# Four token-half seams: the new layer's first weight tile gets its own place and is split ahead of the norm, and the second half's root goes ahead of the second split

## The reference

```python
def rms_norm(x, w=None):
    y = xf * lax.rsqrt(jnp.mean(xf * xf, axis=-1, keepdims=True) + EPS)
def ada_in(x, g, m, s):
    return rms_norm(x, g) * (1 + m[:, 3 * s + 1][:, None, :]) + m[:, 3 * s][:, None, :]
def swiglu(h, w_in, w_out):
    g, u = jnp.split(h @ w_in, 2, axis=-1)
    return (jax.nn.silu(g) * u) @ w_out
...
    for l in range(DEPTH):      # 2; the context stream likewise, with m_ctx
        x = x + 0.5 * ada_gate(m_lat, 0) * swiglu(ada_in(x, norm_w[l, 0], m_lat, 0), ...)
        hl = ada_in(x, norm_w[l, 1], m_lat, 1)
        yc, yl = ab_mixer(...) if l % 2 == 0 else ret_mixer(...)   # DeltaNet || differential attention; retention
        x = x + ada_gate(m_lat, 1) * yl
        x = x + 0.5 * ada_gate(m_lat, 2) * swiglu(ada_in(x, norm_w[l, 2], m_lat, 2), ...)
    return rms_norm(x, final_norm_w)
```

## Time and profile before

| | us |
|---|---|
| median of 3 runs (2037.15 to 2040.97) | 2037.5 |
| the profiled execution: its own time | 2038.63 |
| the profiled execution: span from first to last instruction | 2036.8 |
| PE busy | 1988.5 (98%) |
| DVE busy | 1282.7 (63%) |
| ACT busy | 751.9 (37%) |
| mean granted TensorE clock | 0.989 of full speed |

### The profile page before, as it was taken

One profiled execution on the slowest core, in us unless ns is written; L12 is line 12 of the kernel. 1 busy time (PEld: TensorE's weight loads), 2 busy tenths in 40 slices (PEclk: granted clock), 3 DMA queues, 4 the chain that ended last, 5 costly groups with the idle time before them and its releaser, 6 DMA issues.

```text
span 2036.8 us, 27638 instructions
## 1 busy us (share of the span) xinstructions
PE 1988.5 (98%) x10253; PEld 1687.3 (83%) x10255; DVE 1282.7 (63%) x1840; ACT 751.9 (37%) x990; POOL 109.3 (5%) x165
## 2 busy tenths in 40 slices
PE   9999999999999999999999999999999999989998
PEld 7888888886788888888888888888887888878886
DVE  6877678775648775877677753453346632666666
ACT  5321222345444333332222343212235432746453
POOL 1010011000003200100001000000000000000000
PEclk8999999999999999999999999999999999999999
DMA  8555455521210002555555432352234422044553
GB/s 349 168 198 177 163 202 166 185 96 40 88 68 21 1 22 104 196 186 174 180 193 172 161 123 98 98 176 103 65 101 167 149 98 104 21 165 137 173 187 122
DMA packets 52650, 274.80 MB, mean 135 GB/s; under 512 B 6128, under 2 KB 7472, under 8 KB 34256
## 3 DMA queue, kind: packets, MB, share of 16 engines
q1 hardware_dynamic: 33024, 203.97, 28.8%
q0 software_dynamic: 18960, 68.88, 10.2%
q10 hardware_dynamic: 576, 0.69, 0.1%
HBM read 272.47 MB, written 1.05 MB: 134 GB/s over the span
## 4 chain that ended last, share of the span: by engine, by line
PE 91%; DVE 5%; ACT 3%; issue 1%; DVEq 0%; ACTq 0%
PE ps L1020 15%; PE ps L1022 14%; PE ps L1021 14%; PE ps L1032 8%; PE ps L1250 6%; PE ps L1252 6%; PE ps L1251 6%; PE ps L1033 4%; PE ps L2397 2%; PE ps L2399 2%; PE ps L2398 2%; PE ps L1902 1%; DVE w_lo L682 1%; PE ps L1914 1%; PE ps L2483 1%
## 5 line engine op out<-in xcount | busy, mean ns | idle before, releaser
L682 DVE TENSOR_TENSOR w_lo<-w_raw,w_hi 128x2048 fp32r<-128x2048 f32 (+3 forms) x206 | 420.8, 2043 | 199.9 <-ACT w_hi L461 199.4
L1020 PE MATMUL ps<-h_parts,w_lo 128*128 128x512 f32 (+1 forms) x1424 | 537.1, 377 | 5.4 <-DVE h_parts L841 4.4
L1022 PE MATMUL ps<-h_parts,w_hi 128*128 128x512 f32 (+1 forms) x1424 | 534.3, 375 | 0.0
L1021 PE MATMUL ps<-h_parts,w_hi 128*128 128x512 f32 (+1 forms) x1424 | 534.2, 375 | 0.0
L461 ACT ACTIVATE w_hi<-w_raw 128x2048 fp32r<-128x2048 f32 (+3 forms) x207 | 354.1, 1710 | 451.8 <-PE ps L1252 254.0
L690 DVE SCALAR_TENSOR_TENSOR ada_product<-ada_w,silu_c 128x1024 bf16<-128x1024 f32 x256 | 313.1, 1223 | 20.3 <-DVE ada_product L690 10.5
L1020 PEld LDWEIGHTS ps<-h_parts,w_lo 128*128 128x128 f32 x1424 | 268.4, 188 | 54.8 <-DVE w_lo L682 5.0
L1022 PEld LDWEIGHTS ps<-h_parts,w_hi 128*128 128x128 f32 x1424 | 268.3, 188 | 48.7
L1021 PEld LDWEIGHTS ps<-h_parts,w_hi 128*128 128x128 f32 x1424 | 268.5, 189 | 47.4
L473 ACT ACTIVATE sil<-ps 128x512 f32<-128x512 f32 x66 | 39.5, 598 | 480.5 <-PE ps L1022 480.5
L1250 PE MATMUL ps<-hid_parts,w_lo 128*128 128x512 f32 x468 | 182.1, 389 | 0.0
(11 more groups left out here) (337 smaller groups left out, 2547.7 us busy)
## 6 DMA issues: line engine op xcount, KB each, us to landing
w_raw<-in_w_up SPq DMA_DIRECT2D x88, 1024.0 KB, 4.8
ada_w<-in_ada POOLq DMA_DIRECT2D x128, 512.0 KB, 3.6
w_raw<-in_w_down SPq DMA_DIRECT2D x32, 768.0 KB, 4.2
w_raw<-in_w_down SPq DMA_DIRECT2D x32, 640.0 KB, 3.9
w_raw<-in_w_ret_t SPq DMA_DIRECT2D x16, 1024.0 KB, 4.8
w_raw<-in_w_ab SPq DMA_DIRECT2D x14, 1024.0 KB, 4.8
ada<-in_ada SPq DMA_DIRECT2D x8, 1024.0 KB, 25.4
w_raw<-in_w_ret SPq DMA_DIRECT2D x8, 1024.0 KB, 4.8
```

The lines of the kernel that those rows point to most:

```text
L682: dve.tensor_tensor(w_lo[parts_of(s, slot)][:, 0:elems], w_raw[slot][:, 0:elems], w_hi[parts_of(s, slot)][:, 0:elems].bitcast(F32), ALU.su ...
L1020: pe.matmul(out, lo, rhs_hi(k), start=first and k == 0, stop=False)
L1021: pe.matmul(out, hi, rhs_lo(k), start=False, stop=False)
L1022: mm = pe.matmul(out, hi, rhs_hi(k), start=False, stop=last and k == nk - 1)
```

## The change

The high and low parts of tile s6 + 2 of each seam get the third pair of buffers (`SEAM_FIRST`), so their making no longer waits for PE to leave a slot: `split_hi` waits for `step_done` s − 2 there. That `split_hi` now stands right behind the dummy root that loads ACT's table, ahead of the squares, and that `split_lo` between the second place of half 0 and the reciprocal. In the rest of the seam `low`s and scales alternate from the start. `split_hi` of tile s6 + 3 stands behind the fourth shift instead of the eighth, `split_lo` of it behind the second half's reciprocal instead of ahead of it (at n11 still ahead). On PE the second part of the second half's sum comes one k later.

```diff
+    SEAM_FIRST = tuple(R[name][1] for name in ("diff", "up1a", "up2a", "retg"))
     def parts_of(s, slot):
-        return 2 if isinstance(s, int) and s == 2 else slot
+        return 2 if isinstance(s, int) and s in (2,) + SEAM_FIRST else slot
...
-            act.wait_ge(step_done, s - 1)
+            act.wait_ge(step_done, s - 2 if isinstance(s, int) and s in SEAM_FIRST else s - 1)
...
         act.activation(warm_root[:], vecs[:, 2:3], ACT.Sqrt).then_inc(warmed, 1)
+        split_hi(act, s6 + 2, s6 % 2, ELEMS[s6 + 2])
         for i in range(2):
             act.wait_ge(sq_added, adds_before(norm) + TAIL - 2 + i)
             square(0, i)
         root(0)
-        split_hi(act, s6 + 2, s6 % 2, ELEMS[s6 + 2])
-        for c in range(4):
+        for c in range(3):
             shift(0, c)
         square(1, 0)
+        shift(0, 3)
+        split_hi(act, s6 + 3, (s6 + 1) % 2, ELEMS[s6 + 3])
         shift(0, 4)
-        shift(0, 5)
         square(1, 1)
-        shift(0, 6)
-        shift(0, 7)
-        split_hi(act, s6 + 3, (s6 + 1) % 2, ELEMS[s6 + 3])
+        for c in range(5, KD):
+            shift(0, c)
         root(1)
...
             place(0, i)
+        split_lo(dve, s6 + 2, s6 % 2, ELEMS[s6 + 2])
         dve.wait_ge(mod_ready, k)
         inverse(0)
         scale(0, 0)
         scale(0, 1)
+        low(0, 0)
         dve.wait_ge(step_done, s6 + 1)
         place(1, 0)
         scale(0, 2)
+        low(0, 1)
         scale(0, 3)
-        split_lo(dve, s6 + 2, s6 % 2, ELEMS[s6 + 2])
-        for c in range(4):
-            low(0, c)
-            scale(0, c + 4)
-            if c == 0:
-                dve.wait_ge(step_done, s6 + 2)
-                place(1, 1)
+        low(0, 2)
+        dve.wait_ge(step_done, s6 + 2)
+        place(1, 1)
         for c in range(4, KD):
-            low(0, c)
+            scale(0, c)
+            low(0, c - 1)
+        low(0, KD - 1)
+        if norm == "n11":
+            split_lo(dve, s6 + 3, (s6 + 1) % 2, ELEMS[s6 + 3])
+            inverse(1)
+            return
+        inverse(1)
         split_lo(dve, s6 + 3, (s6 + 1) % 2, ELEMS[s6 + 3])
-        inverse(1)
-        if norm == "n11":
-            return
...
-                        mm = products(pe, ps[:, 2 * slot + u, cols], slot, u * D + k * P, 1, lambda _: h_hi[:, k, cols],
-                                      lambda _: h_lo[:, k, cols], k == 0, k == KD - 1)
+                        mm = products(pe, ps[:, 2 * slot + u, cols], parts_of(s0 + r, slot), u * D + k * P, 1,
+                                      lambda _: h_hi[:, k, cols], lambda _: h_lo[:, k, cols], k == 0, k == KD - 1)
...
-        elif n == 2:
+        elif n == 3:
             pe_seam_sum(pe, norm, 1, s6, 1)
```

More of the change, by code:

```diff
@@ L2429, in gate_body @@
                 for t in range(2):
-                    mm = token_products(pe, ps[:, gate_bank(r) + t, :], slot, r, kc,
+                    mm = token_products(pe, ps[:, gate_bank(r) + t, :], parts_of(s, slot), r, kc,
                                         slice(SEQ + t * P, SEQ + (t + 1) * P))
```

## The result

The changed kernel took 2026.46 us (median of 4 runs, 2024.94 to 2031.3) against 2038.72 us for the kernel before on the same chip: a ratio on record of 0.9936 with a 95% interval of 0.9917 to 0.9955, some 13 us. How the four runs are summed up matters at this size: the two medians differ by 12.3 us, the two means (2038.9 and 2027.3) by 11.6. Two executions of the changed kernel in the later run `again`, of 3310 and 5290 us, are left out throughout. The profiled execution took 2031.3 us, with a span of 2029.5 and a mean granted clock of 0.989; it was the slowest of the four, so the seams have to be read place by place and not from its span.

The account below looks back on a forecast made before the run. It took TensorE (PE), 98% busy, as the bound. Gains of 2.38 (n01), 2.45 (n02), 2.38 (n10) and 2.01 (n11) sum to 9.2 us, from the median of 2037.5 to 2028.3 us; range 2026.4 to 2032.5.

Parts of the forecast that it names:

- (a): ScalarE at each seam: first tile's `split_hi` ahead of the squares costs nothing; 1.8 us without idle time to cover it.
- (b): VectorE at each seam: first tile's `split_lo` between second place and reciprocal costs nothing, 0.2 us to spare at n02.
- Rival 4: Seams, ScalarE: early `split_hi` waits for a late load and holds up the squares; slower, 2044.7 us at 11 us loads; chance 0.04.
- (c): Each seam: second tile's `split_hi` after four shifts; its chain is the new critical piece, PE's second tile at 410.05 at n01.
- Rival 1: VectorE at each seam: alternating scales and `low`s step at 0.51 us, 1.0 us later per seam; time 2032.3 us; chance 0.11.
- (d): Second half of each seam: root and reciprocal earlier (n11 keeps split first), so the spread no longer waits; the split is late next.
- Rivals 2 and 3: 2: stages behind n01 and n02 hand gains back, 2033.1 us, chance 0.05; 3: waits move whole to second tile, 2035, 0.07.
- I give nothing back: Work behind the seams: same waits in the same order, so no part of the seams' gain is subtracted.
- PE alone, 2026.4: All four seams: if the second split's chain were no bound, PE's own work gives 11.1 us, time 2026.4 us.

Follow-up runs that it names:

- again: The changed kernel with no edit, more rounds; ratio 0.9941 to the kernel before, mean 2027.1 us over six executions.
- home: Kernel before with only the third pair of buffers and both early splits of tile s6 + 2, rest of the order kept; ratio 0.9962.
- root: Kernel before with only the second half's root and reciprocal ahead of the second tile's splits, at n01, n02 and n10; ratio 1.0002.
- two: Changed kernel plus a fourth `w_hi`, with the second tile's `split_hi` directly behind the first root; ratio 0.9933 to the kernel before.
- again2: The changed kernel with no edit, run a third time; ratio 0.9949 to the kernel before, mean 2027.8 us over six executions.
- the padded kernels: Three unread matmuls added at the end of n01, in the changed kernel (ratios 0.9967 and 0.996) and in the kernel before (1.0012).
- start: Changed kernel with 18 more dummy matmuls while PE waits for the first loads; ratio 0.9955 to the kernel before, mean 2028.6 us.
- before_copy: The kernel before with no edit, for a second trace and more runs; ratio 0.9991.

## Why the prediction was right and where it was wrong

**(a), (b), the third place at no cost: right.** ScalarE at n02, the kernel after, then the kernel before:

```profile
782.20 1.91 ACT L463 ACTIVATE w_hi<-w_raw 128x2048 fp32r<-128x2048 f32 x1
784.02 0.40 ACT L544 ACTIVATE prod<-x 128x256 f32<-128x256 f32 x1
...
782.49 0.42 ACT L542 ACTIVATE prod<-x 128x256 f32<-128x256 f32 x1 [1.43 <-DVE x L775]
```

The early `split_hi` starts at 782.20 and the square follows directly, at 784.02. On the time scale of the kernel before (1.18 us less there) that is 782.84, where it was 782.49. So the cover was not the 2.46 us that the prediction took from the earlier trace rows, which lie behind that square, but the 1.43 us of idle ahead of it, and the square slips 0.35 us. Nobody waited for it: PE's part of the sum begins at 785.77, the 784.59 of before plus 1.18. The place was misread, the price of nothing holds. Rival 4's allowance was misread with it: from the end of that square, 783.24, to the sum there were 1.3 us left, so a load later by more than that, not by 2.1, would have begun to cost. `split_lo` (786.37, 2.28 us) leaves DVE 0.35 us idle ahead of the reciprocal, against the 0.2 foreseen. Rival 4 did not occur.

**(c), the chain of the second split: right,** to 0.02 us up to the reciprocal, as the comparison at n01 shows. Scales and `low`s in turn start 0.39 to 0.41 us apart: 0.41 and 0.39 in the rows above. Rival 1, at 0.51, is out, and so is the strict rule of the Trainium skill (VectorE: DVE Perf Modes, The DRAIN you can't avoid), by which instructions of 0.48 could not start closer than that. The same page's allowance for an instruction that nothing holds fits.

**(d) and the sizes of the seams: right in kind, 0.4 us too small in all.** The reciprocal's wait is gone, and what is late next is the split: 0.57 us at n02 (0.7 to 1.0 predicted) and 0.67 at n11 (0.4 to 0.7). At n01 and n10, 0.1 to 0.3 was expected and the trace shows none. At n01 the split starts only 0.08 behind the reciprocal, not 0.16, and PE follows its end by 0.05, not 0.1. That makes up the 0.12 to 0.15 us by which each of the first three seams gave more. `home` and `root` show the split between the parts as worked out, and `two` the bound.

**Rivals 2 and 3: out.** No gain is handed back behind a seam: n01's is there in full at 430 us, and what changes from there to 780 (−0.5, +0.6 and +0.9 in three traces of the same kernel) goes either way. None of the waits moved whole to the second tile.

**The step that failed: "I give nothing back", with "PE alone, 2026.4" as the lower end.** The first part took all work outside the seams to keep its time from execution to execution, a term of zero with no spread, and the second made the sum's own bound the bound of the measurement. Neither holds. Outside the seams the traces differ by −3.2 to −0.3 us at the start, −0.5 to +0.9 in attention and DeltaNet and +0.2 to +1.3 at the end, and the changed kernel's sixteen executions go from 2021.7 to 2032.5. The mean of the first four, 2027.3, is no lower than the mean of all sixteen, 2027.4 ± 0.8; it was their median (2026.5), and more so the ratio on record, that came out low. The kernel before has a mean of 2038.5 ± 0.4 over the 42 executions beside `again` and `again2`. The difference is 11.1 ± 0.9 us where 9.22 was forecast: 0.4 is the seams' terms, and 1.5 ± 0.9 lies outside the seams. By this difference the time would be 2026.4, at the lower end of the range and still 1.9 us under the forecast; the record's 2024.5 lies 1.9 lower again, 0.5 by how the means of the first four fell and 1.4 by how they are summed up in the ratio. That is luck, and of a usual size. Single executions scatter by 3.0 us (changed) and 2.5 us (before), so that the difference of two means of four is uncertain by some 2 us. The range should have had that below its 2026.4. The prediction had the number: it put what a measurement can tell at 4.1 us, and left it out of the range.

**What stays open.** Whether the 1.5 us belong to the change at all. The traces don't show them: outside the seams the three of the changed kernel against the two of the kernel before come to a loss of 0.8 us on average, between −3.8 and +1.7. The mean granted clock of all executions does lean the way of the gain, and clear of noise: 0.9883 ± 0.0002 over 42 of the kernel before, 0.9904 ± 0.0004 over the 16 of the changed one. But within one kernel the time falls by 1.5 us for 0.001 of clock, which makes 3.1 us of that difference, and 11.1 less 3.1 is 8.0, less than the seams give. So the mean clock doesn't account for the rest either. The stretches at 1.2 GHz add up to 44.9 and 41.1 us in the two traces of the kernel before, and to 46.5, 40.6 and 39.7 in the three of the changed one; they come and go within one program, and the padded kernels didn't settle it. That the change shifts their odds is a conjecture. That they make up a part of the spread is shown (1.6 us at the start of one trace, 1.0 us in attention).

## What to carry to other kernels

Where one engine is busy 98% and the rest of the program keeps its order, a hand-written chain of starts worked out from rows came true to 0.02 us over nine starts and to 0.14 at its end; compare the same matmul ahead of and behind each place rather than the spans. The uncertainty of the whole time comes from elsewhere, here up to 3 us in a trace outside the edit, in part by the clock, and it belongs in the range even where the edit doesn't touch it. And when a wait for one item goes, name the next one in the same engine's list and give it a place as well: the fourth buffer brought 2.1 us more, and one body's delay behind n11 another 1.7.

## What the runs showed of the hardware

- The granted clock of one and the same single-core program differs between executions: 41.1 to 44.9 us at 1.2 GHz in the kernel before, 39.7 to 46.5 in the changed one, down to 28.9 in `start`. The stretch at 514 us is there in one profile and missing in the next, with the same instructions in the same order ahead of it.
- What such a stretch costs depends on what else sets the pace: nothing in the 10 us from about 19 us on (DMA share 1.01), 1.0 us for 3.4 us in attention (`before_copy` against the first trace of the kernel before), and half its length where PE's own pace, 0.43 us a matmul in place of 0.23, was the limit (1.6 us for the 3.4 from 34.0 in the first profile, 3.2 for the 6.8 up to 37.6 in `two`). Within each kernel the time falls 1.5 us for each 0.001 of mean clock, with 1.2 us of scatter around that.
- ScalarE and VectorE follow each other's semaphores by some 0.03 us here, and an engine follows a step of PE 0.37 to 0.38 us after the start of its last 256-column matmul. With these two, and the rows' steps of one instruction to the next, nine starts of the predicted chain (up to the reciprocal) were met to 0.02 us.
